# A hybrid decoder layer on one core: fourteen projection steps per mixer pass, placed in seven runs between transposes and Gram products, or in two

## What is computed

```
h = h + W_out( sum_i sigmoid(G_i(n)) * P_i(mixer_i(n)) ),  n = RMSNorm(h)
    mixers: A = RWKV-7 time mixing, B = stick-breaking attention,
            C = forgetting attention (FoX) with QK-norm
h = h + HierMoE(RMSNorm(h))     top-1 group, then top-2 SwiGLU experts
```

```
def step(S, inp):
    r_t, w_t, k_t, v_t, kk_t, a_t = inp
    sa = jnp.einsum('bhvk,bhk->bhv', S, -kk_t)
    S = (S * w_t[:, :, None, :]
         + sa[..., None] * (kk_t * a_t)[:, :, None, :]
         + v_t[..., None] * k_t[:, :, None, :])
    return S, jnp.einsum('bhvk,bhk->bhv', S, r_t)
```

## Time and profile before

| | |
|---|---|
| median of 3 runs | 935.89 us (935.33 to 936.1) |
| profiled execution, its own time | 936.31 us |
| its span, first to last instruction | 934.6 us |
| TensorE matmuls busy | 874.3 us, 94% of the span |
| TensorE weight loads busy | 505.8 us |
| VectorE, ScalarE, GpSimd busy | 285.3, 196.8, 100.9 us |
| mean granted TensorE clock | 0.974 |

### The profile page before, as it was taken

One profiled execution on the slowest core, in us unless ns is written; L12 is line 12 of the kernel. 1 busy time (PEld: TensorE's weight loads), 2 busy tenths in 40 slices (PEclk: granted clock), 3 DMA queues, 4 the chain that ended last, 5 costly groups with the idle time before them and its releaser, 6 DMA issues.

```text
span 934.6 us, 16279 instructions
## 1 busy us (share of the span) xinstructions
PE 874.3 (94%) x6948; PEld 505.8 (54%) x6948; DVE 285.3 (31%) x587; ACT 196.8 (21%) x390; POOL 100.9 (11%) x225
## 2 busy tenths in 40 slices
PE   3999999999998999999999999997999957999995
PEld 3878888877776765445454444443445542333331
DVE  3244811312312222452302244333531143222212
ACT  5135111122026111241412121143002220111100
POOL 7720000000003100011000000000000001212121
PEclk9999999999999999999999999998999967999998
DMA  8212136000000000047111112025565077899972
GB/s 228 58 46 88 47 80 193 2 2 3 2 3 1 3 3 25 23 101 199 46 50 32 50 54 68 1 76 177 168 230 227 22 282 281 290 380 386 384 274 110
DMA packets 76135, 109.76 MB, mean 117 GB/s; under 512 B 16891, under 2 KB 61067, under 8 KB 71968
## 3 DMA queue, kind: packets, MB, share of 16 engines
q1 hardware_dynamic: 71296, 93.22, 29.3%
q0 software_dynamic: 4768, 15.52, 5.7%
HBM read 100.32 MB, written 10.50 MB: 119 GB/s over the span
## 4 chain that ended last, share of the span: by engine, by line
PE 90%; DVE 3%; DMA 2%; ACT 2%; issue 1%; SPq 0%; DVEq 0%; POOL 0%; POOLq 0%; ACTq 0%
PE ps L1489 18%; PE ps L1514 10%; PE ps L1841 9%; PE ps L1466 8%; PE ps L1433 8%; PE ps L1793 6%; PE ps L1754 5%; PE ps L1867 5%; PE ps L1471 4%; PE ps L1828 1%; PE ps L1669 1%; PE ps L1737 1%; PE ps L1711 1%; DMA arena<-in_w_p_fox 1%; PE ps L1687 1%
## 5 line engine op out<-in xcount | busy, mean ns | idle before, releaser
L1489 PE MATMUL ps<-arena 128*128 128x512 f32 x304 | 142.9, 608 | 0.0
L1489 PEld LDWEIGHTS ps<-arena 128*128 128x128 f32 x304 | 54.8, 191 | 62.6 <-issue 60.7
L1841 PE MATMUL ps<-arena 128*32 128x512 f32 x624 | 86.0, 598 | 0.1
L1514 PEld LDWEIGHTS ps<-arena 64*64 64x64 f32 x2376 | 73.3, 134 | 23.7 <-issue 13.7
L1514 PE MATMUL ps<-arena 64*64 64x64 f32 x2376 | 80.3, 220 | 1.6 <-ACT arena L780 1.3
L1433 PE MATMUL ps<-arena 128*128 128x264 f32 x320 | 74.8, 393 | 0.6 <-PE ps L1433 0.6
L1433 PEld LDWEIGHTS ps<-arena 128*128 128x128 f32 x320 | 61.2, 193 | 13.5 <-issue 1.8
L1466 PE MATMUL ps<-arena,h 128*128 128x264 f32 x256 | 65.5, 397 | 0.5 <-PE ps L1433 0.5
L1754 PE MATMUL ps<-yT_all,arena 128*128 128x512 f32 x112 | 52.6, 623 | 5.3 <-DMA arena<-in_w_p_fox 5.1
L1793 PE MATMUL ps<-arena 128*128 128x512 f32 x128 | 56.2, 594 | 0.0
L1466 PEld LDWEIGHTS ps<-arena,h 128*128 128x128 f32 x256 | 45.9, 188 | 9.6 <-issue 0.8
(11 more groups left out here) (342 smaller groups left out, 1019.4 us busy)
## 6 DMA issues: line engine op xcount, KB each, us to landing
arena<-in_moe_w_down SPq DMA_DIRECT2D x32, 512.0 KB, 15.9
arena<-in_moe_w_gate SPq DMA_DIRECT2D x13, 1024.0 KB, 11.0
arena<-in_moe_w_up SPq DMA_DIRECT2D x13, 1024.0 KB, 16.3
arena<-in_w_in SPq DMA_DIRECT2D x19, 512.0 KB, 3.9
arena<-in_w_in SPq DMA_DIRECT2D x5, 1024.0 KB, 9.5
h<-in_x SPq DMA_DIRECT2D x8, 512.0 KB, 5.1
arena<-in_w_out SPq DMA_DIRECT2D x1, 4096.0 KB, 14.7
h<-in_w_in SPq DMA_DIRECT2D x3, 1024.0 KB, 5.1
```

The source lines that it names most:

```text
L1489: ins = mm(ps[:, gate_bank(n), :], weights_of_gate(n)[:, c, :], nT[:, c, META:L], start=(c == 0), stop=(c == DC - 1))
L1514: ins = mm(psf[q, 512 * bank + c * CH:512 * bank + (c + 1) * CH], lhs(q, c), rhs(q, c), start=True, stop=True)
L1841: ins = mm(ps[rs, bank, :].rearrange("p (h n) -> p h n", h=2), xgT[:, s, c, rs], w1[ws][:, :, c, :], start=(c == 0), stop=(c == DC - 1))
```

## The change

In the head of each pass TensorE's 14 steps are placed otherwise. Before, there were 2 after the second transpose, 3 after the fourth, 1 after each of the five Gram products and 4 more after the last (`INIT_FILL`). After, there are 5 after the fourth transpose (`TURN_FILL`) and 9 after the last Gram product. Nothing else is edited; the number of steps per pass is the same, and so is `HEAD_FILL`. The list `pe_order` is edited to match.

```diff
--- before.py
+++ after.py
@@ -54,7 +54,8 @@
 EARLY_GATES = 5
 EARLY_SLOTS = 3
 SHIFT_ORDER = (4, 1, 2, 0, 3)
-INIT_FILL = 4
+INIT_FILL = 9
+TURN_FILL = 5
 LEVEL_FILL = 3
 CAP = 96
 NR = NE * CAP // P
@@ -322,7 +323,7 @@
         pe_order = []
         for p_ in range(RC):
             for k_ in range(4):
-                pe_order.append((("tr", p_, k_), {1: 2, 3: 3 + 5}.get(k_, 0)))
+                pe_order.append((("tr", p_, k_), TURN_FILL if k_ == 3 else 0))
             pe_order.append((("init", p_), INIT_FILL))
             for lv_ in range(1, 6):
                 pe_order.append((("H", p_, lv_), 2 + LEVEL_FILL))
@@ -1529,8 +1530,6 @@
                     if k == 2:
                         pe.wait_ge(sem("tr_used"), 4 * p + 1)
                     units(6 * (k % 2), cm(z), idq).then_inc(sem("tr_psum"), 1)
-                    if k == 1:
-                        fill_qkv(2)
 
                 pe.wait_ge(sem("tr_used"), 4 * p + 2)
                 units(6, vsrc, idq, c1=NCH - 1)
@@ -1541,7 +1540,7 @@
                 for q in quads:
                     ins = mm(psf[q.start:q.start + w, 3072 + (NCH - 1) * CH:3072 + NCH * CH], vsrc(q, NCH - 1), ident2[q, :], start=True, stop=True)
                 ins.then_inc(sem("tr_psum"), 1)
-                fill_qkv(3)
+                fill_qkv(TURN_FILL)
                 for k, (lhs, rhs) in enumerate(((Kt, At), (Kt, Rt), (Bt, At), (Bt, Rt), (At, Bt))):
                     if k >= 2:
                         pe.wait_ge(sem("g_used"), 5 * p + k - 1)
@@ -1551,7 +1550,6 @@
                     if k == 1:
                         pe.wait_ge(sem("tr_used"), 4 * p + 4)
                     units(4 + 2 * (k % 2), cm(lhs), cm(rhs)).then_inc(sem("g_psum"), 1)
-                    fill_qkv(1)
                 fill_qkv(INIT_FILL)
                 pe.wait_ge(sem("g_used"), 5 * p + 5)
                 pe.wait_ge(sem("tr_used"), 4 * p + 4)
```

## The result

The changed kernel takes 928.83 us by the median of 5 runs (927.42 to 930.75), the kernel before 935.89: 7.1 us less. The ratio, for which one slow run of before (1040.72 us) is left out, is 0.9931, or 6.5 us less, 95% interval 0.9918 to 0.9943, so 5.3 to 7.7 us less. The forecast was 931.4, range 930.0 to 933.9. The sign, and nearly all that was said of the passes, held; the size did not.

A forecast was written before the change was run, and what follows sets the result against it. TensorE's own sequence was taken as the bound, with time lost between products and steps. Round trips 5.0 plus copy wait 0.3 less new waits 0.85 gave 4.45 us, so a median of 931.4 us, range 930.0 to 933.9.

The forecast's parts named there:

- What bounds the kernel: TensorE's own sequence, filled in the heads of the passes, with 0.33 us lost per run of steps between two products.
- (1): Heads of the passes: of seven runs of steps two are left, saving five times 0.33 = 1.65 us a pass, 5.0 in all.
- rival B: Lost times belong wholly or partly to a product's end, not the change of work, and stay: 936.4 or 934.3 us; 9%.
- (2): First pass, ahead of the inverse: with nine steps TensorE's wait for the predicated copy goes, saving 0.3 us.
- (3): Gram products lose their cover: products 3 and 5 wait for masks, 4 does not; 0.18 to 0.32 us a pass.
- (4): Transposes lose their cover: the third and fourth wait 0 to 0.04 us each for copies.
- The sum: 5.0 + 0.3 - 0.85 = 4.45 us off the profiled 936.31, giving 931.9; from the median 935.89, a forecast of 931.4.
- Rival C: TensorE's clock falls in head stretches that now hold only 64x64 products, making the kernel slower: 942.9 us; 5%.
- A: Transposes and Gram products that waited also lose overlap with the one ahead: 3.6 us in all, giving 934.2; 12%.
- D: More is gained: releases come faster, no product waits, the whole 5.3 us are left: 930.6 us and below; 6%.

The follow-up runs named there:

- turn_only: Kernel before with only the 2 steps behind the second transpose moved behind the fourth, 5 there; single steps behind Gram products stay: 933.04 us, ratio 0.9978.
- more_turns: Changed kernel with its 5 steps behind the transposes spread again, one behind each of the first three and two behind the fourth: 932.71 us, ratio 0.9975.
- three_pairs: Changed kernel with the five Gram products spread over three pairs of PSUM banks instead of two: 927.84 us, ratio to the kernel before 0.9922.
- after_pad49: Changed kernel with 4.91 us of extra products of constants ahead of the first pass: 935.57 us, ratio to the kernel before 1.0001.
- one_lump_pairs: As three_pairs, with the 5 steps behind the transposes joined to the 9 ahead of the inverse, one run of 14: 929.40 us, ratio 0.9935.

## Why the prediction was too small

**What bounds the kernel**: right. The heads became 4.91 us shorter, and the passes as a whole 4.92.

**(1) Round trips, 5.0 us**: right, if slightly small. turn_only took three away (1.01) and more_turns put nine in (3.1); in the second and third head 1.52 us saved and 0.19 of new waits make 1.71 for five, so 0.34 each and 5.1 in all. The Trainium skill (TensorEngine Tiling (Array Packing), Key Properties) has a change of tiling mode drain TensorE, and the runs agree, with the last chunk's 64x16 tiles too. The estimate of 0.1 us a round trip in rival B is a third of what was measured.

**(2) The wait for the predicated copy, 0.3 us**: right, gone in the first pass, whose head lost 0.35 us more than the others.

**(3) and (4) New waits, 0.85 us**: the mechanism was right, the size too large. Gram products 3 and 5 wait, 4 does not, as said; but each by 0.09, the shorter end (release 0.05 us after the mask), where I took the longer. Transposes don't wait. It is 0.19 a pass, 0.57 in all, and three_pairs takes it away whole.

**The sum**: 4.45 forecast for the heads, 4.9 measured. That is 0.5 of the 2.6 us between the forecast of 931.4 and the median of 928.83.

**The step that failed** is the one from the sum to a median: "4.45 us, against the profiled execution's 936.31 ... the forecast for a median is 931.4", with half a microsecond for the spread of the runs. It took for granted that what follows the passes is only moved, and takes as long as before. It doesn't, and this is the other 2 us or so. What the runs show in its place: after_pad49 moves the later stages back by 4.9 us with the heads left as changed, and the kernel loses 6.8 us. The place where it is seen best is the attention stage, with a stretch at the lower clock in some executions (1.66 us each); both profiles of before have it and one of the two of the changed kernel. The later stages, 409.0 to 410.1 us in all, vary too. How the surplus divides between them is not shown. In before the clock is 0.98 from 480 to 560 us, which I could have read there; I looked only into the heads. Rival C asked after the clock, but where the work was changed, and only for a fall.

**Rivals**: A (a product after a wait loses its overlap too) is out: a product after a wait takes 1.05. B is out by turn_only: 1.01 us for three round trips, where it had none, or 0.42 if only the 0.14 goes. D's "more is gained" came true with its mechanism wrong: two products do wait. That its range of 930.6 and below was met is luck.

**Still open**: how the clock comes to fall in that stage. The moment has a part in it. Sorted by the stage's start in the profile, whatever the kernel, the twelve without the gate step have two low stretches at 404.66 us, one at 404.91, none at 405.01, 405.63 and 405.92, one at 406.52, two at 408.89, none at 410.28, one at 410.78, 410.80 and 411.25, and none at 413.07. So the changed kernel has one at 404.91 and none at 405.92, and the padded changed kernel (410.80) has one as the kernel before does (410.78 and 411.25). But 404.91 and 405.01 differ with 0.1 us between them, so the start in the span is not all of it.

The standstills are a suspect: with them filled, three profiles of three are free of low stretches, without them five of twelve. That is no proof, since at a rate of five in twelve three free ones would come by chance one time in fourteen. And they can't be the whole cause. The first low stretch of one_lump_pairs begins at 465.5, 17 us after the last standstill ended (448.18), and directly ahead of it TensorE is recorded as busy throughout, with the many small products of lines 1669 and 1674:

```profile
461.00:465.50 4.50, 4.50 (x26) 3.37 (x26) 0.00 (x0) 0.00 (x1) 0.00 (x0) 1.00 0.04 9
```

## What to carry to other kernels

Where a busy TensorE changes between small tiles and full ones, measure a round trip from starts: here each cost 0.33 to 0.34 us beyond its work. Filling a wait with foreign work pays only where the wait is longer than that; between back-to-back products whose masks take 0.76 us the wait was 0.09. Put the filler in few long runs, at the waits that are long. And before a gain of half a percent is read from two medians, pad the faster kernel by the gain: if later stages have a clock that comes and goes, the padded one shows what was the edit's and what was the moment's.

## What the runs showed of the hardware

- A stage that nobody touched took 112.20, 113.85 or 115.59 us, as the granted clock was at its lower level in no, one or two short stretches of it; one costs 1.65 to 1.70 us. 4.9 us more work ahead of it cost 6.8 us, 1.95 us more cost 0.25 to 0.9. One such stretch followed 4.50 us in which TensorE was recorded as busy throughout.
- Behind products on 64x16 tiles, 64x64 tiles start as late as full-size steps do: 0.22 us after the first of the 64x16 tiles in both cases, and four transposes take 4.57 us to the one and 4.56 to the other. Removing that run of steps saved 0.20 us a pass and not 0.33.
- VectorE's mask of 128x576 ends 2.14 us after its product starts, and the product that waits for it starts 0.05 us later, by the start of its own mask; over two pairs of banks such a row of products loses 0.09 us in 2.10, over three nothing.
